# Eight of the first mixer's ten head turns move into the projection's last chunk, small loads go between weight pieces, and all convolution weights are formed first

## The reference

```
h = rms_norm(x, pre_mix_norm[l]);  proj = h @ w_in[l]
a = neighbourhood_attention(na_q, na_k, na_v, na_rel_bias[l])
b = rms_norm(softmax(q1 k1) v - lam * softmax(q2 k2) v, diff_subln[l]) * keep
c = gqa(rope(rms_norm(gq_q)), rope(rms_norm(gq_k)), gq_v)
d = mla(rms_norm(ml_cq) @ w_uq, rms_norm(ml_ckv) @ w_ukv, rope(ml_kr))
x += rms_norm(concat(a, b, c, d) @ w_o, post_mix_norm)
x += rms_norm((silu(gate) * up) @ w_down, post_ffn_norm)
```

## Time and profile before

| | us |
|---|---|
| median of 3 runs | 2028.98 |
| lowest, highest | 2027.85, 2031.43 |
| the profiled execution, its own time | 2027.56 |
| its span, first to last instruction | 2025.8 |
| PE busy | 1875.1 (93%) |
| PE's weight loads | 1634.8 (81%) |
| DVE busy | 1136.7 (56%) |
| ACT busy | 922.2 (46%) |
| POOL busy | 179.9 (9%) |
| mean granted clock of TensorE | 0.962 |

### The profile page before, as it was taken

One profiled execution on the slowest core, in us unless ns is written; L12 is line 12 of the kernel. 1 busy time (PEld: TensorE's weight loads), 2 busy tenths in 40 slices (PEclk: granted clock), 3 DMA queues, 4 the chain that ended last, 5 costly groups with the idle time before them and its releaser, 6 DMA issues. The chain is left out here.

```text
span 2025.8 us, 28967 instructions
## 1 busy us (share of the span) xinstructions
PE 1875.1 (93%) x11496; PEld 1634.8 (81%) x11496; DVE 1136.7 (56%) x1647; ACT 922.2 (46%) x1267; POOL 179.9 (9%) x213
## 2 busy tenths in 40 slices
PE   4888999898899989899999999999969999989998
PEld 4657999775799978779998879998648998768997
DVE  3665555676655568664445455445655445765443
ACT  3364444445544446555344454435234344564432
POOL 0400000040000001001000000101420010100000
PEclk8989999898999999799999999999979999999999
DMA  5602555550255555324554534454715554435451
GB/s 180 236 5 94 167 186 186 178 183 30 74 186 186 186 176 161 125 84 167 186 187 168 179 109 166 168 206 152 215 49 171 186 187 167 167 109 177 172 206 63
DMA packets 185356, 313.07 MB, mean 155 GB/s; under 512 B 18878, under 2 KB 67572, under 8 KB 185268
## 3 DMA queue, kind: packets, MB, share of 16 engines
q1 hardware_dynamic: 182595, 304.24, 44.1%
q0 software_dynamic: 1376, 4.38, 0.8%
q10 hardware_dynamic: 1296, 3.24, 0.5%
HBM read 309.90 MB, written 1.94 MB: 154 GB/s over the span
## 5 line engine op out<-in xcount | busy, mean ns | idle before, releaser
L1404 DVE TENSOR_TENSOR w_lo<-raw,w_hi 128x2048 fp32r<-128x2048 f32 (+2 forms) x290 | 651.5, 2278 | 307.2 <-ACT w_hi L953 306.4
L953 ACT ACTIVATE w_hi<-raw 128x2048 fp32r<-128x2048 f32 (+2 forms) x290 | 533.3, 1876 | 110.1 <-PE tr L1938 63.8
L1936 PE MATMUL acc<-w_hi,aux_hi 128*128 128x512 f32 x688 | 269.6, 392 | 12.4 <-DVE aux_lo L1896 12.4
L1937 PE MATMUL acc<-w_lo,aux_hi 128*128 128x512 f32 x688 | 268.8, 391 | 0.0
L1938 PE MATMUL acc<-w_hi,aux_lo 128*128 128x512 f32 x688 | 268.2, 390 | 0.0
L1936 PE MATMUL up<-hT_hi,w_hi 128*128 128x256 f32 x864 | 246.3, 285 | 8.1 <-ACT proj L1335 5.1
L1936 PE MATMUL acc<-w_hi,hT_hi 128*128 128x512 f32 (+2 forms) x608 | 238.9, 393 | 8.9 <-DVE w_lo L1404 8.0
L1938 PE MATMUL up<-hT_hi,w_lo 128*128 128x256 f32 x864 | 245.4, 284 | 0.0
L1937 PE MATMUL up<-hT_lo,w_hi 128*128 128x256 f32 x864 | 245.4, 284 | 0.0
L1936 PE MATMUL tr<-hT_hi,w_hi 128*128 128x256 f32 x864 | 244.9, 283 | 0.0
L1937 PE MATMUL tr<-hT_lo,w_hi 128*128 128x256 f32 x864 | 244.5, 283 | 0.0
(11 more groups left out here) (344 smaller groups left out, 2460.4 us busy)
## 6 DMA issues: line engine op xcount, KB each, us to landing
raw<-in_mlp_w_up SPq DMA_DIRECT2D x64, 1024.0 KB, 6.6
raw<-in_mlp_w_down SPq DMA_DIRECT2D x64, 1024.0 KB, 5.4
raw<-in_ffn_w_gate_up SPq DMA_DIRECT2D x88, 512.0 KB, 4.7
raw<-in_ffn_w_down SPq DMA_DIRECT2D x22, 1024.0 KB, 4.9
raw<-in_w_in SPq DMA_DIRECT2D x16, 1024.0 KB, 7.4
raw<-in_sb_w_in SPq DMA_DIRECT2D x12, 1024.0 KB, 6.0
raw<-in_moba_w_in SPq DMA_DIRECT2D x12, 1024.0 KB, 5.5
raw<-in_nsa_w_in SPq DMA_DIRECT2D x10, 1024.0 KB, 5.2
```

Of the source, the lines that this page charges most:

```text
L953: nc.scalar.activation(w_hi[:, p0.slot, 0:p0.floats], raw[:, p0.slot, 0:p0.floats], ACT.Copy)\
L1404: nc.vector.tensor_tensor(w_lo[:, p0.slot, 0:m], raw[:, p0.slot, 0:m], f32(w_hi[:, p0.slot, 0:m]), ALU.subtract).then_inc(sem["lo_ready"], 1)
L1936: nc.tensor.matmul(dst, hi, whi, start=first, stop=False)
L1937: nc.tensor.matmul(dst, hi, wlo, start=False, stop=False)
```

## The change

1. The order of the ten pairs of head tiles is changed, so that the two of the differential attention come last. PE does the first eight (`jobs_early`) after the first piece of the projection's last chunk (`i` = 4), and waits there for the bias tables, for POOL's rotations and for ACT's copies; ACT copies them out before it copies out the chunk. In `mix_A` PE waits for the chunk before the last only, starts score step 0 and 1, and does the last two turns (`diff_jobs`) after step 1; ACT copies them out (`diff_turned`) after the exponentials of step 1.
2. The turn of the later vectors moves from `A_0` to the head of `A_1`, on PE and on ACT.
3. SP issues pieces 0 to 9 in a row, with `first` behind piece 4, the later vectors behind piece 5, the first layer's seven row loads behind piece 7 and its bias behind piece 9. The second layer's seven row loads go out at the end of the first feed-forward, before its bias. The waits for rows count per layer.
4. The three row tensors become one, `first_rows`, and `region` has 1024 more floats in use; both serve as the fifth and the sixth buffer of convolution weights. POOL forms all six weights before the first store.

```diff
 PAIR_STEPS = 20
 DF_FIRST, GQ_FIRST, ML_FIRST = 4, 12, 16
+JOBS_EARLY, JOBS_A = 8, 10
 EARLY = 4
 QUAD = 32
...
         n_second = max(b for _, b in where_second.values())
         region = sb("region", [P, max(2048 + n_first, n_second + 6 * HD2)])
+        REGION_FREE = n_second + 6 * HD2
...
-        gq_gain = sb("gq_gain", [P, 2, 6 * HD])
-        subln = sb("subln", [P, 2, HD])
-        lam_rows = sb("lam_rows", [P, 2, 4 * 32])
+        first_rows = sb("first_rows", [P, 2 * (6 * HD + HD + 4 * 32)])
+        gq_gain = first_rows[:, 0:12 * HD].rearrange("p (l c) -> p l c", l=2)
+        subln = first_rows[:, 12 * HD:14 * HD].rearrange("p (l c) -> p l c", l=2)
+        lam_rows = first_rows[:, 14 * HD:18 * HD].rearrange("p (l c) -> p l c", l=2)
         small = sb("small", [P, 224])
         norm_rstd = small[:, 184:186]
...
-        ROWS_LANDED = 16 * (len(rows) + 1)
+        ROWS_PER_LAYER = len(rows) // 2
+
+        def rows_landed(l):
+
+            return 16 * (1 + ROWS_PER_LAYER * (l + 1))
+
         second_rows = [(nsa_gain[:, 0:HD2], repeated("nsa_q_norm_2", 0, [1, HD2])),
                        (nsa_gain[:, HD2:4 * HD2], repeated("nsa_k_norm_2", 0, [1, 3 * HD2])),
                        (moba_gain[:, 0:HD2], repeated("moba_q_norm_2", 0, [1, HD2])),
...
         lag_weights = [a.rearrange("p (q j c) -> p q j c", q=4, j=LAGS) for a in
-                       [h[:, 0, :], h[:, 1, :], probT[:, :, :].rearrange("p a s -> p (a s)"), post_gain[:, :]]]
+                       [h[:, 0, :], h[:, 1, :], probT[:, :, :].rearrange("p a s -> p (a s)"), post_gain[:, :],
+                        region[:, REGION_FREE:REGION_FREE + 1024], first_rows[:, 0:1024]]]
         all_taps = vecT[:, 2:4, :].rearrange("p a r -> p (a r)").rearrange("p (j s k) -> p s j k", j=LAGS, s=4)
 
...
                 return [(two(col("na_q")), tiles[:, 0:2, :], 1.0), (two(col("na_k")), tiles[:, 2:4, :], 1.0),
-                        (two(col("df_q")), tiles[:, 4:6, :], 1.0), (two(col("df_k")), tiles[:, 6:8, :], 1.0),
                         (two(col("gq_q")), tiles[:, 8:10, :], -float(HD) ** -0.5), (one, tiles[:, 10:11, :], 1.0),
                         (two(2048, 96, 96), tiles[0:96, 11:13, :], -96.0 ** -0.5),
                         (two(2048 + 192, 96, 96), tiles[0:96, 13:15, :], -96.0 ** -0.5),
-                        (ks[0], tiles[0:96, 15:17, :], 1.0), (ks[1], tiles[0:96, 17:19, :], 1.0)]
+                        (ks[0], tiles[0:96, 15:17, :], 1.0), (ks[1], tiles[0:96, 17:19, :], 1.0),
+                        (two(col("df_q")), tiles[:, 4:6, :], 1.0), (two(col("df_k")), tiles[:, 6:8, :], 1.0)]
             qs = [(two(2 * P * j), tiles[:, 2 * j:2 * j + 2, :], 1.0) for j in range(4)]
             if kind == "nsa":
                 return qs + [(two(c), tiles[:, 8 + 2 * j:10 + 2 * j, :], 1.0)
...
-            for at in range(SLOTS):
+            def load_later_vectors():
+
+                load_rows([(0, vec_rows[1], "conv_dw_b_2"), (8, vec_rows[1], "conv_ln_g_2"),
+                           (16, vec_rows[1], "conv_ln_b_2")], "vec_later_landed")
+                pos = A["nsa_cmp_pos_2"][0].rearrange("j l d -> (j l) d")
+                sp.dma_start(vec_rows[1][24:88, :], pos).then_inc(sem["vec_later_landed"], 16)
+                taps = A["conv_dw_w_2"][0].rearrange("j (k c) -> (j k) c", c=P)
+                for half in range(2):
+                    rows_here = VEC_ROWS[2 + half]
+                    sp.dma_start(vec_rows[2 + half][0:rows_here, :], taps[P * half:P * half + rows_here, :])\
+                      .then_inc(sem["vec_later_landed"], 16)
+
+            def load_first():
+
+                sp.dma_start(region[:, 2048:2048 + n_first], A["first"]).then_inc(sem["row_landed"], 16)
+
+            def load_layer_rows(l):
+
+                for dst, src in rows[ROWS_PER_LAYER * l:ROWS_PER_LAYER * (l + 1)]:
+                    sp.dma_start(dst, src).then_inc(sem["row_landed"], 16)
+
+            beside = {SLOTS: load_first, SLOTS + 1: load_later_vectors, SLOTS + 3: lambda: load_layer_rows(0),
+                      SLOTS + 5: lambda: load_bias(sp, 0)}
+            for at in range(SLOTS + 6):
                 load([plan.pieces[at]])
-
-            sp.dma_start(region[:, 2048:2048 + n_first], A["first"]).then_inc(sem["row_landed"], 16)
-            for dst, src in rows:
-                sp.dma_start(dst, src).then_inc(sem["row_landed"], 16)
-            load_rows([(0, vec_rows[1], "conv_dw_b_2"), (8, vec_rows[1], "conv_ln_g_2"),
-                       (16, vec_rows[1], "conv_ln_b_2")], "vec_later_landed")
-            pos = A["nsa_cmp_pos_2"][0].rearrange("j l d -> (j l) d")
-            sp.dma_start(vec_rows[1][24:88, :], pos).then_inc(sem["vec_later_landed"], 16)
-            taps = A["conv_dw_w_2"][0].rearrange("j (k c) -> (j k) c", c=P)
-            for half in range(2):
-                rows_here = VEC_ROWS[2 + half]
-                sp.dma_start(vec_rows[2 + half][0:rows_here, :], taps[P * half:P * half + rows_here, :])\
-                  .then_inc(sem["vec_later_landed"], 16)
-            load([plan.pieces[SLOTS]])
-            load_bias(sp, 0)
-            at = SLOTS + 1
+                if at in beside:
+                    beside[at]()
+            at = SLOTS + 6
             for ph in phases:
                 if ph.kind == "ffn":
                     while at < ph.first:
...
                     if ph.variant == "A" and ph.row == 1 and LAYERS[1:2] == [("A", 1)]:
+                        load_layer_rows(1)
                         sp.wait_ge(sem["x_written"], 4)
                         load_bias(sp, 1)
...
                 quads = c2("quads").unsqueeze(1).unsqueeze(1)
-                nc.gpsimd.tensor_tensor(lag_weights[k % len(lag_weights)], bc(quads, [P, 4, LAGS, QUAD]),
+                nc.gpsimd.tensor_tensor(lag_weights[k], bc(quads, [P, 4, LAGS, QUAD]),
                                         bc(taps, [P, 4, LAGS, QUAD]), ALU.mult).then_inc(sem["quads_ready"], 1)
 
...
                 pool.wait_ge(sem["tap_evac"], n["tap_evac"])
-                for k in range(EARLY):
+                for k in range(CONV_PE):
                     lag_weight(k)
                 pool.wait_ge(sem["pt_evac"], n["pt_evac"] + 2)
...
-                    lag_weight(k)
 
             for ph in phases:
                 if ph.kind == "gemm" and ph.mix is not None and ph.mix.kind == "mixA":
...
+                        for j in range(JOBS_EARLY):
+                            _, dst, scale = jobs_for("A")[j]
+                            evac_job(j, dst, scale, n["pt_ready"])
                     act.wait_ge(sem["piece_used"], pieces[-1][0] + 1)
                     act.wait_ge(sem["rstd_ready"], n["rstd_ready"])
                     nc.scalar.activation(proj[:, 0, n0:n0 + w], sum_bank(ph, i, 0)[:, 0:w], ACT.Copy,
...
-                if ph.l == 0:
-                    vectors_out((1, 2, 3), 2)
                 for t in range(TT):
                     for a, w, dst in ((2048, 256, 12 + t), (2304, P, 14 + t)):
...
+                if ph.l == 0:
+                    vectors_out((1, 2, 3), 2)
                 for k in range(3):
                     act.wait_ge(sem["aux_tr"], n["aux_tr"] + (1 if k < 2 else 2))
...
                 nc.scalar.activation(lam[:, 0:2], lam[:, 2:4], ACT.Exp).then_inc(sem["lam_exp"], 1)
-                for j, (_, dst, scale) in enumerate(jobs_for("A")):
-                    if j == 2:
+
+                def diff_turned():
+
+                    for j in range(JOBS_EARLY, JOBS_A):
+                        _, dst, scale = jobs_for("A")[j]
+                        if j > JOBS_EARLY:
+                            evac_job(j, dst, scale, n["pt_ready"])
+                            continue
                         act.wait_ge(sem["pt_ready"], n["pt_ready"] + j + 1)
                         for a in range(2):
                             ins = nc.scalar.activation(dst[:, a, :], tr[:, j % 2, S * a:S * a + S], ACT.Copy,
                                                        scale=c1("df_scale")[:, a:a + 1])
                         ins.then_inc(sem["pt_evac"], 1)
-                    else:
-                        evac_job(j, dst, scale, n["pt_ready"])
 
                 def pair_out_hi(ks):
                     for k in ks:
...
+                    if i == 1:
+                        diff_turned()
                     if 2 <= i < len(steps) + 2:
                         j = i - 2
                         width = S if steps[j]["diff"] is not None else 2 * S
-                        act.wait_ge(sem["pt_ready"], n["pt_ready"] + 10 + j + 1)
+                        act.wait_ge(sem["pt_ready"], n["pt_ready"] + JOBS_A + j + 1)
                         if j >= 2:
                             act.wait_ge(sem["o_done"], n["o_done"] + j - 1)
                         nc.scalar.activation(probT[:, j % 2, 0:width], tr[:, j % 2, 0:width], ACT.Copy)\
...
-                dve.wait_ge(sem["row_landed"], ROWS_LANDED)
```

(44 more changed lines are left out.)

11 lines of the change are left out of this document (6 added, 5 removed).

## The result

Three rounds of the two kernels side by side gave 2012.59 us after the change (median of 6 runs, 2005.03 to 2017.64) against 2028.41 before (6 runs, 2024.62 to 2031.43). The ratio is 0.9921, with a 95% interval of 0.9897 to 0.9945: 16 us less, between 11 and 21. The prediction was 2001, or 27 less, with a range up to 2012: the sign is right, about 11 us of the gain are missing, and the time lies just outside the range. The profiled execution happens to be the slowest of the six (2017.64, span 2015.8), so only parts of it can be compared with before, not its whole.

A forecast was written before the change was run, and what follows sets the result against it. TensorE, busy 93% of the span, was taken as the bound, so only its waits could pay. Terms -18.5, -3.2, -13 and +7.4 gave -27.3 from 2027.56: 2000.3, about 2001 with the profiled run's lead; range 1991 to 2012.

The forecast's parts named there:

- start: First layer's start: turning vectors after the second chunk and spreading small loads was to save 18.5 us.
- turns: Last projection chunk in both layers: eight turns moved inside it were to save 3.2 us, between 0 and 5.
- convolution: Convolution: all six weights formed before the first store were to save 13 us, at best 14.
- row loads of layer 2: End of first feed-forward: seven row loads ahead of the bias were to cost 7.4 us, bounds 3.3 and 12.7.
- Rival D: Row loads before the second layer's first piece served singly at 13.3 each: 93 instead of 7.4, 2087 us; chance 0.04.
- rival A: Second layer's row loads cost only their issue, the queue having run dry: 3.3 instead of 7.4, 1997 us; chance 0.12.
- -2.1 (...) and -1.1: -3.2 together: From last chunk to score steps: early turns were to save 2.1 us in the first layer, 1.1 in the second.
- POOL issues the fifth group's loads at 1461.90: Convolution: fifth group's loads issued 1461.90 to 1464.2, landing 3.2 after issue, so PE starts that group about 1467.5.
- Rival B: Convolution: POOL's load issues held until DVE's last tap, so the gain is 4.5 to 7, time 2008 us; chance 0.08.
- Rival C: First layer's start: rows or weight pieces land later than wanted, making loads the limit again, 2007 us; chance 0.14.

The follow-up runs named there:

- start_only: Kernel before plus only the change's start, with the second layer's row loads among the first feed-forward's first pieces; 20.7 us less than the kernel before (17.0 to 24.1).
- rows_split: Changed kernel with four of the second layer's seven row loads among the first feed-forward's first pieces, three left before the bias; ratio 0.9882 to the kernel before.
- stacks_first: Changed kernel, row loads among feed-forward's first pieces, all turns at mixer's head, SP's later pieces held behind sixth group's stack loads; repeat 29.2 us under the kernel before.
- rows_in_gap: Changed kernel with the second layer's seven row loads among the first feed-forward's first pieces, not before its bias; ratio 0.9865 to the kernel before.
- gap_again: Second measurement of the changed kernel with the second layer's seven row loads among the first feed-forward's first pieces; 23.9 us less than the kernel before.

## Why the prediction was right and wrong

| us | predicted | measured by its own kernels |
|---|---|---|
| start | -18.5 | -20.7 |
| turns | -3.2 | -0.2, +0.8, +1.0, +2.2, +2.6: mean +1.3 |
| convolution | -13 | -7.9 |
| row loads of layer 2 | +7.4 | +6.1, +7.1 |
| sum | -27.3 | -20.7 |
| the change as a whole | | -16.0, -21.3 |

The measured parts add up to the second measurement of the whole (-21.3), and to the far end of the first's interval (-20.9), with 3 to 4 us of noise on the larger ones. Two terms of the sum failed: the turns (4.5 us short of the forecast) and the convolution (5.1 short). That the whole is off by less than these 9.6 is in part luck, since the start and the row loads gave 3.0 more than forecast.

**Start: right.** The second layer's course as the measure of the first was good. The new wait was 1.87, at the place I named, against the 2.4 in the sum. In after, the chunk was copied out at 88.95 and not at 87. Two things make up most of the 1.8 between: the wait of 2.48 at the fourth chunk, where the second layer of before has 1.93, and a second dip of the clock (58.2 to 61.6), where I had counted 0.8 for one. In start_only's trace the wait is 1.92 and neither dip is there, and it is 20.95 ahead at the first score step.

**Row loads: right.** 8.7 in the trace and 6.1 to 7.1 in the time stand against 7.4, bounds 3.3 and 12.7. The bias's issue time before was the right row to read: it had paid the same price once already. Rival D (93) and rival A (3.3) are both out. rows_split shows that the price grows with how much the loads in front have to move: 2.2 for 48 KB, 8.7 for 288 KB. The Trainium skill (DMA: Bandwidth & Descriptors, "Queues, rings and completion order") has each engine take its ring's descriptors in order. With that rule I had worked out 9.4 from the rows of before; the profiled 8.7 lies between the 7.4 and the 9.4.

**Turns: the step "-2.1 (...) and -1.1: -3.2 together" wrong.** The pieces of the work were right: the last chunk became 5.1 longer, and the first score step follows it after 1.2 and 2.6, where I had 1.35 and 2.8. The two turns between the steps cost 1.3 and 1.6 and not 0.8, so without a long stretch the turns give -2.1 for both layers. What failed is that I priced the mixer behind it at an unchanged clock. In five pairs out of five the mean granted clock is lower with the turns early, by 0.002 to 0.007. A stretch of 34 to 37.5 us at 1.2 GHz stood in five of 16 mixers, and in none of the 16 with the turns at the head; it costs 5.3 or 6.3 each time. For two mixers in an execution that is 2 x 5/16 x 5.7 = 3.5 on average, more than the 2.1. None of the five pairs is clear of noise by itself. By the spread of the executions their mean of +1.3 is known to some 2 us (my estimate): it excludes the forecast -3.2, and not zero. That the loss lies in the long stretches is shown by the traces; why the early turns bring them stays open. I had allowed for dips in the start, where before showed them, and did not ask the same of the mixer, where the trace of before has 17.1 us at 1.2 GHz in either layer.

**Convolution: the step "POOL issues the fifth group's loads at 1461.90" wrong.** I took the first store and the stack loads to keep their times, since nothing of theirs was changed. But the store left 2.3 sooner than before and landed 0.8 later (1440.89 against 1440.07), 9.54 after its issue and not 6.41, and the fifth group's loads were issued at 1464.28, 13.6 after the start of the tap loop and not 8.9. The fifth group began on PE 18.5 after that start, where I had 14.5. stacks_first shows that it is the pieces: with them held back the same code gives the whole 13.9 in the trace. The Trainium skill (DMA: Bandwidth & Descriptors, "Issuing engines are not separate DMA queues") says that transfers of all issuing engines end up on the same 16 DMA engines, and the trace agrees: POOL's store pays for SP's pieces. Rival B didn't come: four loads took 2.29 to issue beside the tap loop, as before.

**Rival C** (the start is loads again) did not come. The small loads went out as I had worked out (vectors from 19.7, rows from 24.1, bias from 36.4), and the 0.6 by which the 2.48 exceeds the second layer's wait is its only trace.

**Chances.** Faster, at 0.91, was right. The range ended at 2012 and the first measurement was 2012.6: the two misses of 5 us have the same sign, and no case of mine held both. The poor ends of my own bounds add up to 9 us less than before, about 2020; I had set that aside with "extremes don't come together". (The last step of the sum is rounded low: 2000.3 and the 1.4 are 2001.7.)

**A better version.** stacks_first_diff_at_head takes 1996.0 us, 0.9842 of the kernel before (0.9828 to 0.9856), and beats both kernels. It is the change, with the row loads in the gap, the two last turns at the head of the mixer, and SP's pieces behind the stack loads.

## What to carry to other kernels

When loads are spread out, ask of every one what is issued right behind it and who waits for that; seven small loads cost 6 to 7 us ahead of a piece that is awaited, and nothing in a gap near the start of the same feed-forward's loads. When a part gets faster, look at what other queues move in those microseconds: here a store from another engine's queue waited for weight pieces that nobody needed yet. Holding those back brought the stage to its full 13.9 in the trace, and 1.6 and 5.9 us in the times of two pairs. And work moved into an engine's waits is not time saved until the clock behind it has been looked at, over several executions and not over one trace.

## What was unexpected

- The mixer's stretch at 1.2 GHz is not fixed: in two traces of one kernel it is 13.7 us (rows_in_gap) and 37.5 (gap_again) in the second layer. Three traces of the same mixer code (gap_again, rows_in_gap, after) show 17.1 + 3.4, 3.4 + 13.7 and 37.5 us in the first layer. What lengthens it is open.
- Two 1 MB pieces on SP's queue doubled the time of a store on POOL's: POOL had it back 9.54 us after it began to issue it with them ahead of it (after), and 4.36 with them held back (stacks_first).
